# Products of constants on TensorE ahead of the recurrence and beside the first steps of the sample's group

## The chip, the cores and the metric

The kernel runs on one core of one Trainium2 chip. The metric is the device time of one execution in microseconds, from a few runs on the same chip; the median of the runs is compared. A profiled execution is separate from those runs and has a time of its own.

## The reference: what is computed

One inference step of an encoder trunk of two layers, for 512 prompt frames and 32 sample frames of 1024 channels that share the weights. Each layer:

```
p = rmsnorm(x) @ w_in                    # 1824 columns, shared by three mixers
A: gated linear recurrence over 256 channels (conv, gates, scan)
B: delta rule with a matrix state, 4 heads of 64 x 64
     S = S*w - (S kk)(kk a)' + v k' ;  y = S r
C: latent attention, 8 heads, latent of 128, one rotary key of 32,
   block-causal for the prompt, 256 cached keys for the sample
x += concat(A, B, C) @ w_out
x += cross-attention into 256 memory tokens, 4 heads of 256
x += squared-ReLU MLP, hidden 4096
```

The end is one more RMSNorm. Outputs are both groups' results and their new states and caches.

## The kernel before

All 544 frames are kept transposed in SBUF, and the big products go by weight tiles of 1024 x 128: a stream of 119 such tiles a layer (`in`, `out`, `mk`, `mv`, `mq`, `mo`, `f1`, `f2`) comes by DMA into a ring of three. ScalarE makes a rounded copy of each tile (`wH`), VectorE the remainder (`wL`), and TensorE takes every product as three (`three`: high by high, low by high, high by low), in two halves of 272 frames (`halves`). The order of each engine's work is written out by hand in the kernel, and semaphores couple the engines.

Between the stages `in` and `out` of each layer lies the stretch that the change touches. There TensorE's program is:

- the values (seven products with `W("uv")`) and the first keys (`project(2)`, `project(3)`, with `W("uk")`), all of plain f32 with up to 512 columns, through banks 4 and 5 of PSUM;
- then `weave(recurrence(), attention())`, which takes a step of the one or of the other by a string of turns.

`attention` runs over 40 units (head h, block b; block 4 of a head is the sample's 32 frames). It starts with two query projections (`project(0)`, `project(1)`: rows whose operands are `ringR`, since the ring's free buffers hold the rounded query weights), and has for each unit u a step with `score(u)` (`akH,aqH` and two more rows) and a step with a further projection and `turn(u - 1)`, the transposes of the normalised weights (`cst,aP`). VectorE and ScalarE rotate and split the queries (VectorE L1920 to L1930, ScalarE `aqH<-hT`) and make the softmax (VectorE L1954 to L1963, ScalarE `aP`).

`recurrence` is mixer B in chunks of 64 frames. The prompt's groups g = 0 to 3 have two chunks each, the sample's group is g = 4 (`NG - 1`) and has one. Two lanes of groups run beside each other; the sample's group is the first of lane 1, and for some steps it is alone. Its steps are `tokens` (eight transposes, L799 to L802), `score_l`, `score_m`, `merge` and `cross` over levels, `solve`, `blocks`, `state`. Ahead of them come five steps of TensorE's turn order in which it has nothing to do for the recurrence (`factor`), while ScalarE takes exponentials (`decays`, `ke`, `afr`, `bf`, `afr`) and VectorE makes the factors with them: L1793 to L1799, with the semaphore `factors` on the last, for which `tokens` waits.

The order string beside the factors, and the helper for a product:

```
BESIDE_FACTORS = ("", "aaa", "aaa", "a", "a")
...
            def mm(out, a, b, start=True, stop=True):
                return e.matmul(out, lhsT=a, rhs=b, start=start, stop=stop)
```

`C(name, a, b)` is a slice of the constants `cst`; `ident` is the identity matrix of 128 x 128 in it, and `reset` a row of zeros and ones, one zero in every 64. Bank 7 of PSUM holds `crossed`, the results of `cross`, later in the same stretch.

Of the kernel before, what the change touches and what calls it, by code (L numbers as in the profile page):

```python
# [19 lines left out]
NG = SEQ // GRP + 1  # L20
# [123 lines left out]
def chunks_of(g):  # L144
    return (0, 1) if g < NG - 1 else (0,)
# [14 lines left out]
def lane_of(g):  # L160
    return int(g in LANES[1])
# [25 lines left out]

BESIDE_FACTORS = ("", "aaa", "aaa", "a", "a")  # L190


def _turns():

    order = ""
    for i in range(ALONE):
        order += "r" + (BESIDE_FACTORS[i] if i < FACTOR_STEPS else "a" * (1 + i % 2))

# [34 lines left out]
def build(nc, wall, lw_d, vec_d, cst_d, x_d, mem_d, mks_d, mvs_d, outs):  # L233
# [5 lines left out]
    with ctx:  # L239
# [97 lines left out]
        def C(name, a, b, rows=slice(0, 128)):  # L337
            return cst[rows, CST[name] + a:CST[name] + b]
# [17 lines left out]
        ident, ones, bones = (C(n, 0, 128) for n in ("ident", "ones", "bones"))  # L356
# [11 lines left out]
        def bank(i, a=0, b=512):  # L368
            return PS[:, i * 512 + a:i * 512 + b]
# [20 lines left out]
        def at(l, name, i=1):  # L390

            return before.get(name, 0) + l * PER_LAYER[name] + i
# [12 lines left out]
        def bank_of(use):  # L405
            i = USES.index(use)
            return 4 + (i % 2 if i < FIRST else use[0] != "s")
# [78 lines left out]
        def akL(l, j):  # L486
            return akL1[:, :] if j else ringR[:, slot_of_out(l, 2), 0:KEYS]
# [12 lines left out]
        def nth(kind, g, b=0):  # L500

            mine = [step for step in REC_STEPS if step[0] == kind]
            return mine.index((kind, g, b)) + 1
# [143 lines left out]
        def _(e):  # L647
            def mm(out, a, b, start=True, stop=True):
                return e.matmul(out, lhsT=a, rhs=b, start=start, stop=stop)  # L649
# [132 lines left out]
            for l in range(DEPTH):  # L782
# [6 lines left out]
                def tokens(g):  # L789
                    x, n = lane_of(g), 64 * len(chunks_of(g))  # L790
                    cols = slice(GRP * g, GRP * g + n)
                    e.wait_ge(s["factors"], at(l, "factors"))
                    i = LANES[x].index(g)
                    if i:

                        p = LANES[x][i - 1]
                        e.wait_ge(s["y_out"], at(l, "y_out", nth("state", p, chunks_of(p)[-1])))
                    for t in range(2):
                        e.transpose(bank(2 * x, 128 * t, 128 * t + 128)[0:n, :], xs[:, 4 + t, cols], ident)  # L799
                        e.transpose(bank(2 * x, 256 + 128 * t, 384 + 128 * t)[0:n, :], afr[:, 0, t, cols], ident)  # L800
                        e.transpose(bank(2 * x + 1, 128 * t, 128 * t + 128)[0:n, :], be[:, t, cols], ident)
                        last = e.transpose(bank(2 * x + 1, 256 + 128 * t, 384 + 128 * t)[0:n, :], ke[:, t, cols],  # L802
                                           ident)
                    last.then_inc(s["tok_T"], 1)
# [4 lines left out]
                def score_l(g):  # L809
                    x = lane_of(g)  # L810
                    e.wait_ge(s["tok_out"], at(l, "tok_out", nth("tokens", g)))
                    for t in range(2):
                        for h, c in quads(g):
                            f = frames(g, c)
                            part(bank(2 * x + h, 128 * t, 128 * t + 128)[rows_of[c], :], bf[rows_of[h], t, f],
                                 afr[rows_of[h], :, t, f])
                    for t in range(2):
                        for h, c in quads(g):
                            f = frames(g, c)
                            last = part(bank(2 * x + h, 256 + 64 * t, 320 + 64 * t)[rows_of[1 - c], :],  # L820
                                        afr[rows_of[h], 0, t, f], bf[rows_of[h], t, f])
                    last.then_inc(s["score_l"], 1)

                def score_m(g):
                    x = lane_of(g)
                    e.wait_ge(s["score_l_out"], at(l, "score_l_out", nth("score_l", g)))
                    for t in range(2):
                        for h, c in quads(g):
                            f = frames(g, c)
                            last = part(bank(2 * x + h, 128 * t, 128 * t + 128)[rows_of[c], :], kf[rows_of[h], t, f],  # L830
                                        afr[rows_of[h], :, t, f])
                    last.then_inc(s["score_m"], 1)

                def cross(g, b):
                    x = lane_of(g)
                    e.wait_ge(s["merge_out"], at(l, "merge_out", nth("merge", g, b - 1)))
                    if nth("cross", g, b) > 1:

                        e.wait_ge(s["cross_out"], at(l, "cross_out", nth("cross", g, b) - 1))
                    for w in range(4):  # L840
                        for c in chunks_of(g):
                            r = rows_of[c]
                            last = part(crossed(x, 64 * w, 64 * w + 64)[rows_of[1 - c], :], LG[x][r, w, 0:64],
                                        XX[x][r, 0, w, :])
                    last.then_inc(s["cross"], 1)
# [70 lines left out]
                def state(g, c):  # L916
# [11 lines left out]
                            last = part(o[:, 384 + 64 * t:448 + 64 * t], src[r, t, :], rp[r, c, t, :], False)  # L928
                    last.then_inc(s["state_mm"], 1)

                def recurrence():
                    for kind, g, b in REC_STEPS:
                        if kind == "tokens":
                            tokens(g)
                        elif kind == "score_l":
                            score_l(g)
                        elif kind == "score_m":
                            score_m(g)
                        elif kind == "cross":
                            cross(g, b)  # L940
                        elif kind == "merge":
                            merge(g, b)
                        elif kind == "solve":
                            solve(g)
                        elif kind == "blocks":
                            blocks(g)
                        elif kind == "state":
                            state(g, b)
                        yield
# [49 lines left out]
                def score(u):  # L999
                    h, b = UNITS[u]  # L1000
                    if u == 0:
                        e.wait_ge(s["marks"], at(l, "marks"))
                    if b == 0:
                        e.wait_ge(s["q_out"], at(l, "q_out", 2 * h + 2))
                        e.wait_ge(s["k_out"], at(l, "k_out", 2 * h + 2))
                    wait_bank(e, l, ("s", u))
                    j = h % 2
                    if b < 4:
                        o, q, keys, rows = bank(bank_of(("s", u)), 0, 128 * b + 128), slice(128 * b, 128 * b + 128), \
                            slice(0, 128 * b + 128), slice(0, MKD)  # L1010
                    else:
                        o, q, keys, rows = bank(bank_of(("s", u)), 0, KEYS - SEQ)[0:DEC, :], slice(SEQ, T), \
                            slice(SEQ, KEYS), slice(0, QKD)
                    mm(o, aqH[rows, j, q], akH[rows, j, keys], True, False)
                    mm(o, aqH[0:QKD, j, q], akL(l, j)[0:QKD, keys], False, False)
                    mm(o, aqL[0:QKD, j, q], akH[0:QKD, j, keys], False, True).then_inc(s["a_score"], 1)
# [37 lines left out]

                def attention():

                    e.wait_ge(s["cq_lo"], at(l, "cq_lo"))
                    for p in range(2):
                        project(p)
                        yield  # L1060
                    for u, (h, b) in enumerate(UNITS):
                        score(u)
                        if u >= 2 and UNITS[u - 2][0] % 2:
                            weigh(u - 2)
                        yield
                        if h + 1 < HEADS and b < (2 if h % 2 == 0 else 4):
                            project(4 * (h + 1) + b)
                        if u in NORM_UNITS:
                            norm_early(NORM_UNITS.index(u))
                        if u:  # L1070
                            turn(u - 1)
                        yield
                    turn(len(UNITS) - 1)
                    weigh(len(UNITS) - 2)
                    yield
                    weigh(len(UNITS) - 1)
# [1177 lines left out]
```

## Time and profile before

| what | value |
|---|---|
| median of 3 runs | 1940.93 us (1940.87 to 1943.75) |
| the profiled execution's own time | 1937.82 us |
| its span, first to last instruction | 1935.7 us |
| mean granted TensorE clock | 0.966 of full speed |
| TensorE busy (matmul) | 1813.7 us (94%) |
| VectorE busy | 1020.1 us (53%) |
| ScalarE busy | 724.9 us (37%) |
| GpSimd busy | 105.2 us (5%) |

The columns of TensorE's rows are start, busy time, engine, line, operands and tiles; the clock of a stretch stands as a share of full speed (1.00 is 2.4 GHz, 0.50 is 1.2 GHz). A product of plain f32 stands in the trace as two matmul rows. Line L649 is that of the helper `mm`, so products are told apart by their tiles. Times are from the span's start. Layer 0's stretch between `in` and `out` runs from 129 to 335 us, layer 1's from 1081 to 1287 us.

### The profile page before, as it was taken

The page shows a single profiled execution, that of the slowest core. Times are in us where ns is not written, and L with a number is a line of the kernel's source. Part 1 is how long each engine was busy: PE and PEld are TensorE (multiplying, and loading weights), DVE is VectorE, ACT ScalarE, POOL GpSimd, SP SyncE. Part 2 cuts the span into 40 slices and gives each one's busy share as a digit, 9 for nine tenths or more (in the row PEclk, how much of TensorE's full clock was granted, in tenths as well). Part 3 has the DMA queues.
Part 4 walks back from the last instruction along what each step waited for, and adds up shares of the span by engine and source line. Part 5 has one row for each costly group of instructions (what it writes and reads, how often), then busy time and mean ns, then how long its engine had stood idle before and what let it go on. Part 6 is the DMA issues. An engine that isn't in the chain of part 4 may idle for free.

```text
span 1935.7 us, 37571 instructions
## 1 busy us (share of the span) xinstructions
PE 1813.7 (94%) x16534; PEld 1699.3 (88%) x16534; DVE 1020.1 (53%) x1741; ACT 724.9 (37%) x1268; POOL 105.2 (5%) x108
## 2 busy tenths in 40 slices
PE   5996988999999999999999789889999999999997
PEld 5975777999889999999999567779987999999996
DVE  6677665554435544344367776655443455353533
ACT  4434555463334212121335355554433422121212
POOL 2020000200010000000100100001000100000001
PEclk9997998999999999999999789999999999999998
DMA  5200000553122222222221000133510222222221
GB/s 218 75 10 1 4 24 25 194 173 116 34 77 77 88 89 87 90 86 91 84 77 55 8 3 2 35 111 119 198 46 32 80 95 88 88 88 88 88 88 58
DMA packets 38593, 149.51 MB, mean 77 GB/s; under 512 B 4384, under 2 KB 4544, under 8 KB 36768
## 3 DMA queue, kind: packets, MB, share of 16 engines
q1 hardware_dynamic: 36288, 131.05, 20.4%
q0 software_dynamic: 2144, 16.06, 2.2%
q8 instruction: 131, 2.15, 0.5%
q14 instruction: 30, 0.25, 0.0%
HBM read 139.68 MB, written 7.41 MB: 76 GB/s over the span
## 4 chain that ended last, share of the span: by engine, by line
PE 85%; DVE 7%; ACT 4%; issue 1%; POOL 1%; DMA 1%; DVEq 0%; ACTq 0%; SPq 0%; POOLq 0%
PE PS L649 78%; PE PS L787 5%; PE PS L1026 1%; DVE stat L1954 1%; ACT hH L1166 1%; ACT aP L1166 1%; POOL sq L575 1%; DVE rs L1921 0%; DVE hT L1920 0%; PE PS L1122 0%; DVE hL L1607 0%; DVE hT L1923 0%; ACT akH L1166 0%; ACT L1166 0%; DVE kf L1780 0%
## 5 line engine op out<-in xcount | busy, mean ns | idle before, releaser
L649 PE MATMUL PS<-hH,wH 128*128 128x272 f32 x2272 | 492.1, 298 | 33.7 <-DMA cst<-cst_in 16.9
L649 PE MATMUL PS<-hH,wL 128*128 128x272 f32 x2272 | 476.7, 291 | 0.0
L649 PE MATMUL PS<-hL,wH 128*128 128x272 f32 x2272 | 476.0, 291 | 0.0
L1593 DVE TENSOR_TENSOR wL<-ring,wH 128x1024 fp32r<-128x1024 f32 x238 | 301.0, 1265 | 216.9 <-ACT wH L1166 216.6
L649 PEld LDWEIGHTS PS<-hH,wH 128*128 128x128 f32 x2272 | 361.5, 190 | 50.5 <-issue 19.1
L1166 ACT ACTIVATE wH<-ring 128x1024 fp32r<-128x1024 f32 x238 | 249.8, 1051 | 333.8 <-PE PS L649 333.8
L649 PEld LDWEIGHTS PS<-hH,wL 128*128 128x128 f32 x2272 | 362.4, 191 | 0.0
L649 PEld LDWEIGHTS PS<-hL,wH 128*128 128x128 f32 x2272 | 360.3, 191 | 0.0
L649 PE MATMUL PS<-hidH,wL 128*128 128x272 f32 x1024 | 212.0, 288 | 0.0
L649 PE MATMUL PS<-hidH,wH 128*128 128x272 f32 x1024 | 211.7, 288 | 0.0
L649 PE MATMUL PS<-hidL,wH 128*128 128x272 f32 x1024 | 211.1, 288 | 0.0
L1619 DVE TENSOR_TENSOR xT<-PS,xT 128x544 f32<-128x544 f32 x96 | 69.4, 723 | 241.8 <-PE PS L649 241.6
L649 PEld LDWEIGHTS PS<-hidH,wH 128*128 128x128 f32 x1024 | 161.0, 188 | 0.0
L649 PEld LDWEIGHTS PS<-hidL,wH 128*128 128x128 f32 x1024 | 160.9, 189 | 0.0
L649 PEld LDWEIGHTS PS<-hidH,wL 128*128 128x128 f32 x1024 | 159.8, 189 | 0.0
L1166 ACT ACTIVATE hidH<-hid 128x544 fp32r<-128x544 f32 x64 | 42.2, 659 | 281.2 <-DVE hid L2085 281.2
L575 POOL TENSOR_TENSOR sq<-sq 128x544 f32<-128x544 f32 x49 | 68.1, 1389 | 1113.3 <-ACT sq L1166 1113.3
L2083 DVE TENSOR_TENSOR hid<-PS,rs 128x544 f32<-128x544 f32 x64 | 46.3, 724 | 114.3 <-PE PS L649 106.2
L1166 ACT ACTIVATE sq<-xT 128x544 f32<-128x544 f32 x56 | 36.8, 657 | 178.9 <-DVE xT L1619 174.3
L1954 DVE TENSOR_REDUCE stat<-PS 128x1 f32<-128x256 f32 (+5 forms) x120 | 55.0, 458 | 71.9 <-PE PS L649 70.3
L1166 ACT ACTIVATE aP<-PS,stat 128x128 f32<-128x128 f32 (+4 forms) x80 | 41.4, 517 | 80.1 <-DVE stat L1955 79.8
L1602 DVE SCALAR_TENSOR_TENSOR hL<-xT,vec,hH 128x544 fp32r<-128x544 f32 x48 | 43.1, 921 | 11.7 <-ACT hH L1166 11.5
(320 smaller groups left out, 2554.9 us busy)
## 6 DMA issues: line engine op xcount, KB each, us to landing
ring<-wall SPq DMA_DIRECT2D x238, 512.0 KB, 3.3
lw<-lw_in POOLq DMA_DIRECT2D x2, 2240.0 KB, 10.2
xT<-x_in SPq DMA_DIRECT2D x4, 544.0 KB, 7.2
y_out<-hT SPq DMA_DIRECT2D x8, 272.0 KB, 2.1
mem<-mem_in POOLq DMA_DIRECT2D x2, 1024.0 KB, 5.0
mks<-mks_in POOLq DMA_DIRECT2D x2, 1024.0 KB, 10.2
mvs<-mvs_in POOLq DMA_DIRECT2D x2, 1024.0 KB, 13.3
memk_out<-mkp POOLq DMA_DIRECT2D x2, 1024.0 KB, 6.1
```

Source lines behind the costliest of these rows:

```text
L575: e.tensor_tensor(sq[:, 0, :], sq[:, 0, :], sq[:, 1, :], ALU.add).then_inc(s["sq_added"], 1)
L649: return e.matmul(out, lhsT=a, rhs=b, start=start, stop=stop)
L787: return e.matmul(out, lhsT=a, rhs=b, start=start, stop=True, skip_group_check=True)
L1026: last = e.transpose(bank(6, 128 * j, 128 * j + 128), aP[:, u % 2, 128 * j:128 * j + 128], ident)
L1166: return e.activation(out, in_, f, **kw)
L1593: tt(wL[:, n % SPLIT], ring[:, n % RING], plain(wH[:, n % SPLIT]), ALU.subtract).then_inc(w_lo, 1)
L1602: stt(hL[:, k, :], xT[:, k, :], V(l, gain, k), plain(hH[:, k, :]), ALU.mult, ALU.subtract)\
L1619: tt(xT[:, k, :], ps, xT[:, k, :], ALU.add).then_inc(evac["dve"], 1)
L1954: link(e.reduce_max(stat[0:n, 16 + u % 2:17 + u % 2], bank(scores, 0, nk)[0:n, :], AX))
L2083: tt(m, ps, rs, ALU.mult).then_inc(evac["dve"], 1)
```

## The change

A helper `keep_busy(n)` issues n products of `ident` with the 512 columns of `reset` into bank 7. They wait for nothing and signal nothing, and nobody reads their result. They stand at these places of each layer, on TensorE alone: five ahead of the first query projection, three ahead of `score(0)`, two ahead of `score(2)`, eight ahead of `tokens` of the sample's group, one ahead of `score(3)`, two ahead of `score(4)`, and two ahead of `score_m` of the sample's group: 23 products a layer, 46 in all.

```
+KEEP_BUSY = {0: 3, 2: 2, 3: 1, 4: 2}
...
+                def keep_busy(n):
+
+                    for _ in range(n):
+                        mm(bank(7), ident, C("reset", 0, 512))
+
                 def recurrence():
                     for kind, g, b in REC_STEPS:
+                        if (kind, g) == ("score_m", NG - 1):
+                            keep_busy(2)
                         if kind == "tokens":
+                            if g == NG - 1:
+                                keep_busy(8)
                             tokens(g)
...
                 def attention():
 
+                    keep_busy(5)
                     e.wait_ge(s["cq_lo"], at(l, "cq_lo"))
                     for p in range(2):
                         project(p)
                         yield
                     for u, (h, b) in enumerate(UNITS):
+                        if u in KEEP_BUSY:
+                            keep_busy(KEEP_BUSY[u])
                         score(u)
```

The first place is TensorE's program of layer 0 where the weave begins: `lw` is the last key product, `ringR` the first query projection. Before:

```order
L649 MATMUL PS<-ckv,lw 128x512
L649 MATMUL PS<-ckv,lw 128x32
L649 MATMUL PS<-lw 128x256
L649 MATMUL PS<-ringR 128x272
L649 MATMUL PS<-cqL,ringR 128x272
```

And now:

```order
L651 MATMUL PS<-ckv,lw 128x512
L651 MATMUL PS<-ckv,lw 128x32
L651 MATMUL PS<-lw 128x256
L651 MATMUL PS<-cst 128x512 x5
L651 MATMUL PS<-ringR 128x272
L651 MATMUL PS<-cqL,ringR 128x272
```

Five products (the rows with `cst` alone) stand between the keys and the projections; nothing else has moved.

The second place is TensorE's program of layer 0 from the turn of unit 1 (`cst,aP`, two blocks) to `score_m` of the sample's group (`afr,kf`); `cst,xs` to `cst,ke` are its `tokens`, `afr,bf` and `bf,afr` its `score_l`. Before:

```order
L1026 MATMUL PS<-cst,aP 128x128 x2
L799 MATMUL PS<-cst,xs 64x128
...
L802 MATMUL PS<-cst,ke 64x128
L649 MATMUL PS<-akH,aqH 128x512
...
L1026 MATMUL PS<-cst,aP 128x128 x3
L787 MATMUL PS<-afr,bf 64x128 x4
L787 MATMUL PS<-bf,afr 64x64 x4
L649 MATMUL PS<-akH,aqH 32x288
L649 MATMUL PS<-ringR,aqH 32x288
L649 MATMUL PS<-akH,aqL 32x288
L787 MATMUL PS<-afr,kf 64x128 x4
```

And now:

```order
L1037 MATMUL PS<-cst,aP 128x128 x2
L651 MATMUL PS<-cst 128x512 x8
L801 MATMUL PS<-cst,xs 64x128
...
L804 MATMUL PS<-cst,ke 64x128
L651 MATMUL PS<-cst 128x512
L651 MATMUL PS<-akH,aqH 128x512
...
L1037 MATMUL PS<-cst,aP 128x128 x3
L789 MATMUL PS<-afr,bf 64x128 x4
L789 MATMUL PS<-bf,afr 64x64 x4
L651 MATMUL PS<-cst 128x512 x2
L651 MATMUL PS<-akH,aqH 32x288
...
L651 MATMUL PS<-akH,aqL 32x288
L651 MATMUL PS<-cst 128x512 x2
L789 MATMUL PS<-afr,kf 64x128 x4
```

Here too the old rows keep their order; eight, one, two and two products stand between them.

## Rows read from the trace of the kernel before

**Rows 1.** Stretches: length, busy us of PE, PEld, DVE, ACT, POOL; granted clock.

```profile
129.00:174.70 45.70, 27.33 (x126) 18.04 (x125) 37.56 (x68) 19.02 (x41) 7.66 (x8) 0.66 0.03 8
174.70:327.30 152.60, 136.97 (x2537) 112.00 (x2536) 95.47 (x283) 81.18 (x223) 1.16 (x2) 0.97 0.05 14
...
1081.40:1126.90 45.50, 27.16 (x125) 17.86 (x123) 37.57 (x68) 19.02 (x41) 7.67 (x8) 0.66 0.03 8
```

**Rows 2.** PE's waits by releaser, 129 to 163 us: total, times, longest.

```profile
PE PS L649 <- DVE ringR L1948: 4.8, 1, 4.8
PE PS L649 <- DVE aqL L1930: 2.5, 1, 2.5
PE PS L649 <- ACT aP L1166: 1.4, 1, 1.4
```

**Rows 3.** PE's waits by releaser, 163 to 175 us.

```profile
PE PS L799 <- DVE afr L1799: 7.2, 1, 7.2
PE PS L787 <- DVE P L1808: 1.5, 1, 1.5
PE PS L649 <- ACT aP L1166: 0.6, 1, 0.6
```

**Rows 4.** Stretches, columns as in rows 1: the waits, and what lies between.

```profile
129.20:137.50 8.30, 8.30 (x22) 2.90 (x20) 7.96 (x8) 4.76 (x9) 5.56 (x7) 1.00 0.13 44
137.50:142.30 4.80, 0.01 (x2) 0.04 (x1) 4.72 (x9) 1.40 (x3) 2.10 (x2) 0.76 0.00 0
142.30:156.30 14.00, 9.73 (x36) 8.24 (x36) 9.50 (x25) 6.58 (x13) 0.00 (x0) 0.50 0.00 1
163.50:167.10 3.60, 3.60 (x14) 2.79 (x14) 2.88 (x7) 1.07 (x2) 0.00 (x0) 0.50 0.02 5
167.10:170.80 3.70, 1.60 (x23) 0.85 (x23) 3.09 (x9) 1.79 (x5) 0.00 (x0) 0.96 0.00 0
170.80:174.10 3.30, 3.30 (x23) 2.49 (x23) 2.26 (x8) 1.47 (x5) 0.00 (x0) 0.50 0.00 0
```

**Rows 5.** Timeline of PE: start, busy us, line, tiles, count, wait before.

```profile
129.19 4.73 PE L649 MATMUL PS<-lw,ckv 128*128 128x512 f32 x10
133.85 1.98 PE L649 MATMUL PS<-lw 128*128 128x512 f32 x4
...
174.89 0.29 PE L649 MATMUL PS<-cqL,ringR 128*128 128x272 f32 x1
...
181.27 2.07 PE L649 MATMUL PS<-ckv,lw 128*128 128x512 f32 x2
183.13 0.63 PE L1026 MATMUL PS<-cst,aP 128*128 128x128 f32 x2
```

**Rows 6.** The chain of waits, 142 to 175 us, in order of time.

```profile
142.29 1.71 PE PS L649 x6
...
147.82 0.89 PE PS L649 x3
...
149.82 1.05 ACT ke L1166
...
154.04 0.46 ACT aP L1166 x2
...
170.61 1.08 PE PS L787 x8
...
173.27 1.47 PE PS L787 x16
```

**Rows 7.** Stretches where the clock is low later, columns as in rows 1.

```profile
181.00:184.30 3.30, 3.30 (x10) 1.95 (x9) 2.00 (x7) 1.83 (x5) 0.00 (x0) 0.50 0.00 0
...
324.00:327.80 3.80, 2.55 (x38) 2.02 (x35) 0.91 (x4) 1.41 (x6) 0.54 (x1) 0.99 0.05 17
327.90:341.20 13.30, 12.58 (x41) 9.29 (x38) 8.71 (x14) 10.99 (x16) 0.54 (x1) 0.50 0.11 41
...
1287.00:1290.00 3.00, 3.00 (x14) 3.00 (x15) 1.42 (x3) 2.99 (x6) 0.00 (x0) 0.50 0.00 0
```

## Prediction

> **What bounds the kernel now.** I read the stretches first, to see where TensorE is not full; then its waits there and who ended them; then its timeline, for what a product costs at either clock; and last the chain of waits through the stretch.
>
> TensorE is busy for 94% of the span, and nearly everywhere it is the bound. The reader should see the exception: in the 45.7 us between the stage `in` and the middle of the weave it is busy for 27.3 us only, at a mean granted clock of 0.66, while VectorE is busy for 37.6 us; layer 1 has the same stretch with the same numbers, 45.5 us and 0.66 [rows 1]. From there on, TensorE is busy for 137 of 152.6 us at 0.97.
>
> In that stretch five waits matter: 4.8 us for the keys' remainders (VectorE L1948), 2.5 us for the queries' (L1930), 1.4 us for a softmax [rows 2], 7.2 us for the last factor (L1799) and 1.5 us for L1808 [rows 3]. The clock tells the rest. In the 8.3 us of f32 products before the first wait it is 1.00; in the wait it falls, and it stays at 0.50 (1.2 GHz) over the whole of 142.3 to 156.3 us, also while TensorE works 9.7 of 14 us, and on through the 7.2 us wait. It rises to 2.4 GHz only at 167.1 us, after 3.6 us of closed work, is lost again at 170.8 us after a stretch with 1.6 us of work in 3.7, and is back at 174.1 us [rows 4]. So about 20 us of work run at half speed. Some of it lies on the chain that ends the stretch, and that part alone is worth anything.
>
> **The price of a product.** An added product is f32 with 512 columns and is two rows. Ten such rows last from 129.19 to the next start at 133.85 us, 0.466 each, so a product costs 0.93 us at 2.4 GHz. Two such rows at 1.2 GHz last from 181.27 to 183.13 us, so it costs 1.86 us there [rows 5]. 46 products are then 43 us of TensorE at full clock. They have cover only as far as TensorE would have waited.
>
> **Step 1, five products in the first wait.** 5 x 0.93 = 4.65 us in a wait of 4.8 us [rows 2] that starts while the clock is 1.00. VectorE's chain to L1948 needs nothing of TensorE, so the first projection starts as before, at 142.3 us; cost nothing. The gap left is about 0.1 us, so the clock has no wait to fall in.
>
> **Step 2, from there to `tokens`, at full clock.** The six matmuls of the first projection take 1.71 us on the chain [rows 6], 0.285 each with their overlap. At full clock a 272-column row follows the next in 0.125 us instead of 0.227 (the start at 174.89 has neighbours at that distance, its own length is 0.29 [rows 5]), so they end about 0.8 us earlier. The three rows of `score(0)`, 0.89 us on the chain [rows 6], give 0.2 to 0.3 more: 1.0 us. That is the start of ScalarE's exponentials. They and the softmax behind them run from 149.8 to 154.5 us without a gap that TensorE ends [rows 6], and VectorE takes the factors without a wait: no further gain, no loss. So `factors` and with it `tokens` come at 162.5 us instead of 163.5 us. Cover for the other products here: three (2.8 us) in the wait of 2.5 us, which grows to about 3 since the projections end sooner; two (1.9 us) in the wait of 1.4 us plus 1.0 us that the rows ahead save; eight (7.44 us) in the wait of 7.2 us. TensorE reaches these eight about 1.9 us earlier than before and `factors` only 1.0 us earlier, so the wait would be about 8.1 us, and 0.6 us is spare. Cost nothing, unless the clock is low.
>
> **Step 3, the sample's first steps at full clock.** `tokens` takes 0.9 instead of 1.7 us, ending at 163.4. One product brings 164.3, `score(3)` (512 columns) 165.0, the turn of unit 2 165.4, `score_l` 166.0; ScalarE's copies of the tokens are ready by 164.8. Two products follow, to 167.9; `score(4)` needs a softmax that would be ready at about 166.9, so here 1.0 us of fill lies on TensorE's own chain. `score(4)` ends at 168.3, two more products at 170.2. L1808, for which `score_m` waits, follows the softmax of unit 3 through VectorE and would now end at about 168.9 instead of 170.6 us [rows 6]: fill costs 1.2 us here. `score_m` starts at 170.2 instead of 170.6 us, only 0.4 us sooner. From there to the end of the first `merge` the old kernel needs 174.7 - 170.6 = 4.1 us, nearly all at 0.50 [rows 4, 6]; at full clock the eight, four and three rows and the sixteen of the merge are some 1.9 us shorter, of which VectorE's L1815 between them leaves 1.8. Gain at that point: 0.4 + 1.8 = 2.2 us.
>
> **The sum.** 2.2 us a layer, in step with what stands behind it, since TensorE is the bound there [rows 1]; two layers give 4.4 us. Against the profiled execution's 1937.82 us that is 1933.4 us. The runs' median lies 3.1 us above the profiled one, so the same sum against 1940.93 us gives **1936.5 us**.
>
> Bounds of what I can't read: the clock after 175 us. It falls again at 181.0 us, for 3.3 busy us [rows 7], which costs 1.6 us; at 327.9 us, where f32 products and the first weight tiles run at 0.50 for 12.6 busy us, against 3.0 us in layer 1 [rows 7]. Half of the difference is 4.8 us on paper, 2.4 us by what the gaps between the products give back. The change moves the work against these falls without a plan. Each can go or come: from 2.4 us lost to 1.6 + 2.4 = 4.0 us won. I take 0, since the layers show both cases, and keep these ends for the range.
>
> **A rule that speaks against it.** The clock is lost in this kernel without any long wait too: at 170.8 us after 1.6 us of work in 3.7 us, and at 327.9 us after 2.6 us in 3.8 [rows 4, 7]. This is what the Trainium skill says on its page "TensorE: Matmul & The Clock Gate", section "A second HAM failure mode: psum-queue depth-cycling": frequent short idle pieces between groups of matmuls let the clock swing, though no single wait is long. By that rule the added products hold the clock only while they stand close, and step 3's gain shrinks. It is the second case below. The trace agrees so far that short waits cost the clock at 170.8 us.
>
> **The rivals.**
> - *The clock is held up to `tokens` but not in the sample's steps.* For it: the fall at 170.8 us, and that the small products there are of 64 x 64. Against it: with five added products the stretch from 162.5 to 170.2 us has no wait above 0.3 us. Then step 2's 1.0 us stays, and step 3 loses its 1.8 us and pays 1.2 us of fill, less the 0.6 us that `tokens` and `score_l` save: about 0.6 us a layer, 1939.7 us.
> - *The later falls go too.* 1.6 us twice, or the 2.4 us of layer 0's end once, on top of the forecast: 1932.5 to 1934.5 us. For it: the falls depend on where the thin pieces come, and these move. Against it: the pieces behind 175 us are unchanged.
> - *The products do not hold the clock* (the other side). Their operands are an identity and ones; no row shows such a product at length. If only useful data counted, the clock would fall during the first wait as now. Price: five products end at about 144.3 instead of 142.3 us (+2.0), three take 5.6 us in 2.5 (+3.1), two take 3.7 in 1.4 (+2.3), eight 14.9 in 7.2 (+7.7 and the lateness of the 7.4 before it), five more 9.3 us over 2.1 us of waits (+7.2): about 22 us a layer, 1985 us; if the fill itself raises the clock after some us, a third of it, about 1955 us. It decides at the first projection: at 1.2 GHz there, this case holds. Against it: f32 products of the same shape hold 1.00 over 8.3 us [rows 4]. The same page says, in "What's actually happening", that the gate goes by how busy the array has been, which would rule this case out.
> - *The later falls turn out worse*: layer 1's end comes to look like layer 0's, +2.4 us in a layer or both, and one more fall: 1937 to 1943 us.
>
> **Chances.** Forecast 0.50 (its own range 1934 to 1939 us), first rival 0.20, later falls go 0.20, no hold 0.03, later falls worse 0.07. A measurement here can tell 0.2%, 3.9 us, from no change: below 1937.05 is faster, above 1944.8 slower. The forecast lies just inside faster: 0.37 of its 0.50; with 0.20 of the good case and a little of the bad, 0.58. Slower: 0.03, 0.02 of the last and as much for what I overlook, 0.07. Same: the rest, 0.35. The range leaves out the no-hold case and the tails: 1932 to 1941 us.
>
> **What would show it.** In the changed profile: granted clock 1.00 from 129 to at least 170 us (and 1081 to 1122); the first projection at 142.3 us still; `tokens` at 162.5 us; `score_m` at 170.2 us released by nothing but TensorE's own row; the first merge ending at 172.5 us; each added product at 0.93 us. Wrong, if the clock is 0.50 at the first projection, if `tokens` does not come sooner (then VectorE, not TensorE, sets all of it), or if the 2.2 us of the stretch is gone by the first `out` tile.

## The result, and the profile after

| | median | runs | ratio to before, 95% interval |
|---|---|---|---|
| before | 1942.34 us | 6 (1939.64 to 1946.28) | |
| changed | 1929.22 us | 6 (1925.53 to 1997.16) | 0.9933 (0.9916 to 0.9950) |

13.1 us are gained (0.7%), where 4.4 us were forecast, and 1929.2 us lies below the stated range. Of the 13.1 us, 1.4 are a kernel before that is slower in these six runs than in the three that the forecast started from (1940.93 us). The execution of 1997.16 us, which was also the first one profiled, had a granted clock near 0.85 over most of its span; the profile read here is that of the first run below (e1), the same kernel at 1924.83 us, with a span of 1922.7 us and a mean clock of 0.990. It is the fastest of the four profiles of the changed kernel that are used here (the others took 1928.4 to 1932.8 us), which agree up to the middle of the weave and differ behind it.

The stretch between `in` and the weave of the changed kernel, with the columns of [rows 1]:

```profile
129.00:171.80 42.80, 39.46 (x164) 20.05 (x164) 36.84 (x66) 18.56 (x39) 7.66 (x8) 1.00 0.03 9
171.80:328.40 156.60, 137.61 (x2573) 111.91 (x2568) 101.16 (x295) 87.42 (x234) 1.16 (x2) 1.00 0.05 17
1074.60:1117.40 42.80, 39.48 (x165) 20.06 (x165) 36.98 (x67) 18.55 (x39) 7.67 (x8) 1.00 0.03 9
```

The clock is 1.00 in both layers' stretches, where [rows 1] have 0.66, and in this profile it is 1.00 to the end of layer 0's weave as well. Its waits from 129 to 172 us, against [rows 2, 3]:

```profile
PE PS L651 <- ACT aP L1180: 1.3, 2, 1.0
PE PS L801 <- DVE afr L1813: 1.1, 1, 1.1
PE PS L651 <- issue: 0.9, 2, 0.5
```

Of some 18 us of waits 3 are left. The timeline of TensorE, the added products (rows `cst` alone, two rows each) and their neighbours:

```profile
137.31 4.46 PE L651 MATMUL PS<-cst 128*128 128x512 f32 x10
142.15 0.37 PE L651 MATMUL PS<-ringR 128*128 128x272 f32 x1 [0.39 <-issue]
...
154.21 7.03 PE L651 MATMUL PS<-cst 128*128 128x512 f32 x16
162.30 0.30 PE L801 MATMUL PS<-cst,xs 128*64 128x128 f32 x1 [1.05 <-DVE afr L1813]
...
167.98 1.88 PE L651 MATMUL PS<-cst 128*128 128x512 f32 x4
169.79 0.65 PE L789 MATMUL PS<-afr,kf 64*64 64x128 f32 x8
...
172.29 0.39 PE L651 MATMUL PS<-ringR 128*128 128x272 f32 x1
```

Sixteen rows take 7.03 us, so a product costs 0.88 us. The first projection starts at 142.15 us, `tokens` at 162.3, `score_m` at 169.8, and the first merge is over at 172.3 us. The forecast had 142.3, 162.5, 170.2 and 172.5 us. So its steps 1 to 3 came out within 0.4 us, and the missing 9 us lie elsewhere.

### The profile page after: what moved, and what is told of

Same layout as the page of the kernel before. It is cut to its first block, busy times and chain, and to the rows that moved or that the text cites. A ratio compares the mean times of both kernels' runs of the same rounds, so it can differ in the third digit from the quotient of the medians.

```text
span 1995.0 us, 37755 instructions
## 1 busy us (share of the span) xinstructions
PE 1911.0 (96%) x16626; PEld 1758.6 (88%) x16626; DVE 1020.3 (51%) x1741; ACT 725.8 (36%) x1268; POOL 105.2 (5%) x108
## 4 chain that ended last, share of the span: by engine, by line
PE 89%; DVE 4%; ACT 4%; issue 1%; POOL 1%; DMA 0%; DVEq 0%; SPq 0%; ACTq 0%; POOLq 0%
PE PS L651 82%; PE PS L789 5%; PE PS L1037 1%; ACT hH L1180 1%; POOL sq L577 1%; DVE stat L1968 1%; PE PS L1136 0%; DVE hL L1621 0%; DVE rs L1935 0%; DVE hT L1934 0%; ACT aP L1180 0%; ACT L1180 0%; POOL msq L629 0%; DVE wL L1607 0%; DMA mem<-mem_in 0%
## 5 line engine op out<-in xcount | busy, mean ns | idle before, releaser
L651 PE MATMUL PS<-hH,wH 128*128 128x272 f32 x2272 | 508.6, 307 | 32.2 <-DVE hL L1616 23.0
L651 PE MATMUL PS<-hH,wL 128*128 128x272 f32 x2272 | 488.7, 298 | 0.0
L651 PE MATMUL PS<-hL,wH 128*128 128x272 f32 x2272 | 488.3, 298 | 0.0
L651 PEld LDWEIGHTS PS<-hH,wH 128*128 128x128 f32 x2272 | 372.1, 194 | 51.9 <-issue 20.5
L651 PEld LDWEIGHTS PS<-hH,wL 128*128 128x128 f32 x2272 | 370.3, 193 | 0.0
L651 PEld LDWEIGHTS PS<-hL,wH 128*128 128x128 f32 x2272 | 369.3, 193 | 0.0
L651 PE MATMUL PS<-hidH,wH 128*128 128x272 f32 x1024 | 216.6, 294 | 0.0
L651 PE MATMUL PS<-hidL,wH 128*128 128x272 f32 x1024 | 216.4, 293 | 0.0
L651 PE MATMUL PS<-hidH,wL 128*128 128x272 f32 x1024 | 216.2, 294 | 0.0
L2097 DVE TENSOR_TENSOR hid<-PS,rs 128x544 f32<-128x544 f32 x64 | 46.4, 725 | 125.4 <-PE PS L651 116.8
L1968 DVE TENSOR_REDUCE stat<-PS 128x1 f32<-128x256 f32 (+5 forms) x120 | 54.9, 458 | 78.5 <-PE PS L651 77.2
L1616 DVE SCALAR_TENSOR_TENSOR hL<-xT,vec,hH 128x544 fp32r<-128x544 f32 x48 | 43.2, 922 | 11.6 <-ACT hH L1180 11.4
```

What stands on the lines that cost most here:

```text
L1616: stt(hL[:, k, :], xT[:, k, :], V(l, gain, k), plain(hH[:, k, :]), ALU.mult, ALU.subtract)\
L1968: link(e.reduce_max(stat[0:n, 16 + u % 2:17 + u % 2], bank(scores, 0, nk)[0:n, :], AX))
L2097: tt(m, ps, rs, ALU.mult).then_inc(evac["dve"], 1)
```

## The experiments

In all of them the kernel before ran beside the others on the same chip. Three points of TensorE's program serve as marks in every layer: the starts of `score` of unit 8 and of unit 22 (three rows each, the first `akH,aqH`, with 512 columns for unit 8 and 384 for unit 22), and the start of the first weight tile of stage `out`. Each is counted from the first row `lw,ckv` at the end of stage `in`, called the stage's end below.

**e1, the change again.**

> The change as it is, once more, for a second set of times and another profile. Theory A (the gain sits in the stretch from 129 to 175 us and its twin, and was mis-sized there): the first merge of the sample's group ends over 5 us earlier than before's 174.7 us, and the rest of each layer is as long as before. Theory B (the stretch gives about 2.2 us a layer as worked out, the rest comes from falls of the clock after 175 us that no longer happen): the merge ends near 172.5 us, and the lowered pieces after it (before: 181, 300, 311, 328 and 356 us in layer 0) are fewer. Both: ratio 0.993.

Measured: 1929.7 us, 0.9935 (0.9918 to 0.9952). Theory A falls: the merge ends at 172.3 us. B is borne out in this profile: of the stretches at 0.50 behind 175 us that the first profile of before has in layer 0, those at 181 [rows 7], 300 and 311 us are absent, and up to there only the one at 328 us is left.

**e2, e3 and e4, parts of the change.** e2:

```
-KEEP_BUSY = {0: 3, 2: 2, 3: 1, 4: 2}
+KEEP_BUSY = {0: 3, 2: 2}
...
-                        if (kind, g) == ("score_m", NG - 1):
-                            keep_busy(2)
```

> Leaves out the five products beside the sample's steps (one, two and two). Theory A: tokens come at 162.5 us; by my sum the five cost 2.2 us of fill and bring 1.8 us, so about the same gain as the whole change, within 1 us a layer. Theory B: if the clock is lost in the sample's steps the later falls are as before, and the ratio goes back to about 0.998.

Measured: 0.9995 (0.9980 to 1.0011). The eighteen products ahead of `tokens` hold the clock and bring `tokens` forward exactly as in e1 (33.14 us behind the stage's end), and the first merge ends 0.5 us behind e1's in layer 0 and 0.9 us in layer 1 (43.7 and 44.1 us behind the stage's end, against 43.2), still 1.4 to 1.9 us sooner than in the kernel before. Yet the kernel is no faster than before. Its profile shows why:

```profile
162.00:165.00 3.00, 1.49 (x22) 0.88 (x21) 2.45 (x7) 1.74 (x5) 0.00 (x0) 1.00 0.00 0
165.00:168.30 3.30, 1.75 (x15) 1.00 (x15) 3.08 (x8) 1.47 (x5) 0.00 (x0) 1.00 0.00 0
168.50:185.40 16.90, 16.84 (x94) 12.33 (x94) 9.36 (x28) 6.20 (x18) 0.00 (x0) 0.50 0.00 1
```

TensorE works about half the time from 162 to 168 us, the clock goes to 1.2 GHz, and it stays there for 17 us in which TensorE is busy without a pause. In layer 1 it is the same, and unit 22 comes at 110.5 us in both layers.

e3 is the other half:

```
+KEEP_BUSY = {3: 1, 4: 2}
...
-                            if g == NG - 1:
-                                keep_busy(8)
...
-                    keep_busy(5)
```

> Keeps only the five products beside the sample's steps and leaves out the eighteen ahead of tokens. Clock at 1.2 GHz until about 167 us as before, tokens at 163.5 us. Theory A: no gain, 0.5 to 1.5 us a layer of fill on TensorE's chain, ratio 1.000 to 1.0015. Theory B: if these five are what keeps the clock later on, ratio 0.996 or below.

Measured: 0.9964 (0.9950 to 0.9977). Five products a layer, which make the first merge no earlier than before (it ends 45.5 and 46.4 us behind the stage's end, against 45.5), win some 7 us. Theory A gave them a loss. The clock comes back 37 and 39 us behind the stage's end, inside the sample's steps, and is not lost in them again; unit 22 comes at 107.9 and 108.7 us.

e4 leaves out the eight products alone:

```
-                            if g == NG - 1:
-                                keep_busy(8)
```

> Leaves out the eight products in the 7.2 us wait for the factors alone. The clock holds until about 155 us, is lost in the wait, and the sample's steps run at 1.2 GHz until it rises: Theory A: the 1.0 us of step 2 stays, the five later products cost up to 2 us each pair at the low clock, ratio 0.999 to 1.003. Theory B: the later falls come back too, the same ratio or worse.

Measured: 0.9968 (0.9955 to 0.9981). Both theories expected a slower kernel than this. The clock is lost in the wait for the factors (at 0.50 from 159 to 169 us) as expected, but `tokens` keeps its gain (33.13 us), and the sample's steps have no low stretch of 17 us. Unit 22 comes at 109.0 us.

**e5, e6, e7 and e12, more profiles of the unchanged kernels.**

> The kernel before, unchanged, for another profile. Theory B1 (the later falls of the clock are placed by the way the clock rises at the end of the low stretch, so the same in every execution): low near 181, 300 and 311 us in layer 0 and at the same distances behind tokens in layer 1, as in the first profile. Theory B2 (they are chance, and the first profile was unlucky): other places, fewer of them.

> The changed kernel, unchanged, for another profile. Theory B1: no low clock between 129 and 328 us or 1 to 2 pieces at places that differ from profile to profile. Theory B2: 2 to 4 pieces in each layer, at places that differ.

> As the one before: a third profile of the changed kernel, to see whether the places of the low pieces repeat.

> The kernel before, for a third profile: whether the low stretch of 17 us from 170 to 188 us is the usual case (then score of unit 22 starts 112.0 us behind the stage's end) or the short one of the first profile is (108.9 us).

The second profile of the kernel before (e5, 1943.71 us), stretches with the columns of [rows 4]:

```profile
163.50:167.10 3.60, 3.60 (x28) 2.75 (x28) 2.85 (x7) 1.07 (x2) 0.00 (x0) 0.56 0.02 5
167.10:170.60 3.50, 1.30 (x22) 0.73 (x15) 2.92 (x8) 1.79 (x5) 0.00 (x0) 0.92 0.00 0
170.80:174.20 3.40, 3.40 (x27) 2.58 (x24) 1.92 (x7) 1.64 (x5) 0.00 (x0) 0.50 0.00 0
174.20:181.00 6.80, 6.80 (x47) 5.91 (x46) 3.44 (x10) 2.01 (x7) 0.00 (x0) 0.50 0.00 0
181.00:187.60 6.60, 6.60 (x32) 4.04 (x28) 3.71 (x11) 2.83 (x7) 0.00 (x0) 0.54 0.00 0
...
1126.50:1143.50 17.00, 16.94 (x99) 12.43 (x98) 9.49 (x27) 6.44 (x19) 0.00 (x0) 0.52 0.00 1
```

Up to 170.8 us this is the picture of [rows 4]; but where the clock came back at 174.1 us there, here it stays at 0.50 to 187.7 us, in both layers. The third profile (e12, 1947.79 us) has the same 17 us in both layers. So four of the six layers profiled have it, and the one profile that the forecast was worked from, the fastest of the three at 1937.82 us, has it in neither.

| us from the end of `in` | score of unit 22 | first `out` tile |
|---|---|---|
| before, first profile, layers 0 and 1 | 109.0, 108.9 | 206.2, 205.4 |
| before, e5 | 112.0, 112.0 | 208.2, 209.5 |
| before, e12 | 112.1, 112.0 | 209.7, 209.4 |
| changed, e1, e6, e7, e14 (8 layers) | 105.5 in each | 199.0 to 203.2 |

The rows for unit 22 in layer 0 of the first profile of before, then of e5, then of e1 (the stage ends at 129.19, 129.20 and 129.17 us):

```profile
238.16 0.42 PE L649 MATMUL PS<-akH,aqH 100*128 100x384 f32 x1
```

```profile
241.23 0.42 PE L649 MATMUL PS<-akH,aqH 100*128 100x384 f32 x1
```

```profile
234.72 0.42 PE L651 MATMUL PS<-akH,aqH 100*128 100x384 f32 x1
```

None of these four profiles of the changed kernel has a low clock between 129 and 188 us or at that place of layer 1; the eight layers reach unit 22 within 0.04 us of each other. Further on neither B1 nor B2 holds. The changed kernel too has low pieces at three places of a layer, near 240, 295 to 302 and 305 to 312 us by the times of layer 0: e6 has the later two in both layers, e14 one of them in layer 0 and both in layer 1, e7 all three in layer 0 and the first in layer 1, e1 none. The kernel before has two or three such pieces in each of its six layers, in the second layers of e5 and e12 one of them at another place.

**e8, fewer products in the sample's steps.** e2 with the two products ahead of `score_m` kept.

> Keeps the eighteen products ahead of tokens and the two ahead of score_m, and leaves out the three beside unit 3 and 4. The wait before score_m was where the clock was lost without any of the five (thin from 165 to 168.5 us). If the two alone hold the clock, the low stretch of 17 us goes, and the ratio is 0.993 or better, since about 1 us of fill a layer is saved. If they don't (the work of 163 to 166 us stays thin), the clock is lost near 168 us in most executions and the ratio is 0.997 to 1.000.

Measured: 1929.3 us, 0.9935 (0.9918 to 0.9952), unit 22 at 104.8 us in both layers: two products in place of five save 0.8 us a layer and hold the clock here. The same kernel again, as e16:

> The kernel of e8 again: 0.9935 as before, 0.7 us a layer ahead of e14 up to unit 22, which the noise of the times hides.

Measured: 1931.22 us, 0.9935 (0.9921 to 0.9950). In layer 0 the clock is low from 167 to 170 us, and unit 22 comes at 106.2 us. Over the twelve layers profiled with this pair alone (e8, e11, e13, e15, e16, e18) that happened in four, layer 0 each time, and it costs 1.4 us; with all five products it happened there in none of ten (e1, e6, e7, e14, e17). The three further products buy this for 0.8 us a layer, which comes to about nothing on the mean (1.4 us in four of twelve layers is 0.5 us).

**e9, as many products, an eighth of the columns.**

```
-                        mm(bank(7), ident, C("reset", 0, 512))
+                        mm(bank(7, 0, 64), ident, C("reset", 0, 64))
```

> The 23 products of a layer stay where they are, but with 64 columns instead of 512: as many instructions, an eighth of the work, at most 0.25 us each. If it is the closed work that holds the clock, it is lost in the first wait and in the 7.2 us wait as before, and the time is that of before: ratio 0.999 to 1.002. If some activity in the waits is enough, whatever its amount: tokens 33.1 us behind the last stage's end and 0.993.

Measured: 1936.95 us, 0.9987 (0.9966 to 1.0007), with times from 1931 to 1947 us. Two stretches of its profile:

```profile
140.60:154.00 13.40, 11.00 (x50) 10.27 (x49) 9.72 (x25) 6.58 (x13) 0.00 (x0) 0.53 0.01 2
154.00:161.00 7.00, 3.11 (x15) 2.92 (x16) 6.95 (x8) 1.78 (x5) 0.00 (x0) 0.50 0.00 0
```

As many instructions stand at the same places, and the clock is lost at 141 us: it is the products' length that counts, not their presence. Whether the short ones do nothing at all is not shown. Neither layer of this profile has the low stretch of 17 us, the median lies 5.5 us below that of the kernel before beside it, and the interval of the ratio allows both no gain and 0.3%.

**e10, the pair behind the thin piece.** e2 and

```
-KEEP_BUSY = {0: 3, 2: 2}
+KEEP_BUSY = {0: 3, 2: 2, 5: 2}
```

> The eighteen products ahead of tokens, none in the sample's thin piece, and two just behind it (ahead of score(5)). If the two products ahead of score_m work by keeping the clock from being lost there, these come too late: lost near 168 us. If all that counts is to get it back, the low stretch of 17 us shrinks to 3.4 or 7 us. Ratio between those of e2 and e8: 0.996 to 0.999. If the clock plays no part in the step, 0.999 to 1.000 as e2.

Measured: 0.9959 (0.9942 to 0.9976), between e2 and e8. The clock is lost near 167 us in layer 0 and at the same place of layer 1, the low stretch lasts 6.8 us instead of 17, and unit 22 comes at 109.0 and 108.7 us, where e2 has 110.5. The added rows run at the low clock:

```profile
170.61 3.62 PE L651 MATMUL PS<-cst 128*128 128x512 f32 x4
```

In this profile the clock is back behind the long products in both layers, where in e2 it stayed low through 17 us of small work without a pause. That e10's ratio lies below e2's agrees; two layers of each are little evidence for more. To keep the clock, as e8 does, is worth 4 us a layer more up to unit 22.

**e11, e13, e15: two later waits.** To e8 come one product ahead of `blocks` of group 0 and one ahead of `norm_squares`, each in a wait of TensorE for ScalarE, into a bank that is free there:

```
+                        if (kind, g) == ("blocks", 0):
+                            keep_busy(1)
...
                     if i == 0:
                         wait_bank(e, l, ("g", 1))
+                        keep_busy(1, 5)
```

> As e8 (eighteen ahead of tokens, two ahead of score_m), and one product in each of two later waits: ahead of blocks of group 0 (1.5 us wait for ScalarE's copy) and ahead of norm_squares (1.7 us). Each product lies in its wait and costs nothing. If the falls near 243 us and near 300 us come from these two waits, they go: about 1.4 us each in the executions that have them, 2 to 5 us for the kernel, ratio 0.991. If the thin work around them is what does it, no change against e8: 0.9935.

> The kernel of e11 again, beside the others on the same chip. If the two later products win what e11 showed: ratio 0.991, and below e14's and e16's by 0.002 or more; no low clock near 240 us and near 300 us in the profile. If e11 was chance: as e16.

> The changed kernel, for comparison on the same chip: ratio 0.9935. Its profile: score of unit 22 at 105.5 us behind the stage's end, the later falls at 240, 300 or 310 us in some layers.

> As e8 with the one product ahead of blocks of group 0, without the one ahead of norm_squares. If each later fall hangs on the wait beside it: the fall near 240 us is gone (unit 23 at 7.76 us behind unit 22 in every layer), those near 300 us stay, ratio between e13's and e16's.

Measured: e11 1923.65 us, 0.9909 (0.9887 to 0.9931); e13, the same kernel, 1923.35 us, 0.9892 (0.9875 to 0.9909); on the same chip e14, the changed kernel, 1929.21 us, 0.9919 (0.9902 to 0.9935), and e15 1927.13 us, 0.9916 (0.9898 to 0.9934). The wait ahead of `norm_squares` in e14 and the stretches around it in layer 0:

```profile
293.29 1.10 PE L651 MATMUL PS<-rstd_early,cst 128*128 128x256 f32 x4 [1.67 <-ACT rstd_early L1180]
```

```profile
291.00:294.00 3.00, 1.33 (x12) 1.09 (x7) 1.32 (x5) 1.54 (x5) 0.00 (x0) 1.00 0.00 0
294.00:297.50 3.50, 3.50 (x54) 3.00 (x52) 0.42 (x1) 1.37 (x4) 0.00 (x0) 0.55 0.02 5
```

and in e13:

```profile
292.33 1.07 PE L651 MATMUL PS<-cst 128*128 128x512 f32 x2
294.08 1.13 PE L651 MATMUL PS<-rstd_early,cst 128*128 128x256 f32 x4 [0.67 <-ACT rstd_early L1183]
```

```profile
291.00:294.00 3.00, 2.40 (x47) 1.51 (x41) 1.65 (x6) 2.36 (x7) 0.00 (x0) 1.00 0.02 5
294.00:297.50 3.50, 3.42 (x59) 2.80 (x60) 0.45 (x2) 1.76 (x6) 0.00 (x0) 1.00 0.00 0
```

One product of 0.88 us in a wait of 1.67 us keeps the clock there. The eight layers profiled with it (e11, e13, e17, e18) have no low piece between 285 and 320 us or at that place of layer 1; of the twelve that have the five products or the pair in the sample's steps but nothing in either later wait (e1, e6, e7, e14, e8, e16), nine have one. e15, which fills only the earlier wait, was expected to keep these pieces and has none in its one profile. But three of its six times lie at 1924.5 to 1925.3 us with a mean clock of 0.989 (the profiled one is of these) and three at 1928.9 to 1931.9 us with 0.983, as if the pieces came in half of its executions; no profile of a slower one shows it. For the fall near 240 us the evidence is thin: of those twelve layers one first and three second layers have it, and of the ten with the product ahead of `blocks` none at the place itself; e18 has one some 20 us further on, in layer 1.

**e17 and e18.** The changed kernel with all 23 products and the two later ones (e17), beside the kernel of e13 (e18).

> The changed kernel with all its 23 products a layer, and the two later ones of e13. In the profiles so far the three products that e13 leaves out cost 0.75 us a layer, but without them the clock was lost near 167 us in 3 of 10 layers, at 1.4 us. So against e18 about 0.3 us a layer slower, within the noise: ratio 0.989 to 0.991, no low clock between 129 and 320 us.

> The kernel of e13, a third time, beside e17: ratio 0.989 to 0.991, low clock near 167 us in some layer, none near 240 and 300 us.

Measured: 1923.93 us, 0.9902 (0.9886 to 0.9917), and 1925.55 us, 0.9906 (0.9892 to 0.9920). They can't be told apart, as expected. Not as expected, e17 has one low piece in the sample's steps of layer 1, at 1122 us, a place where no other profile with its products has one; unit 22 comes at 106.5 us there instead of 105.5. So the five products don't hold the clock there in every execution. Both kernels beat the kernel before by 1.0%; on one chip (e13 against e14) the two later products and the leaner pair together beat the changed kernel by 5.9 us.

## Why the prediction was wrong

*Steps 1 and 2* held: 142.15 against 142.3 us, 162.3 against 162.5 us. A product took 0.88 us, not 0.93. The rival that such products don't hold the clock is refuted by the clock of 1.00 over 42.8 us.

*Step 3* held in its numbers. The gain at the merge is 2.35 us against the first profile. The fill delays `score_m` by 1.1 us against e2 (40.6 against 39.5 us behind the stage's end; the forecast had 1.2), and even so the merge ends 0.5 to 0.9 us sooner than in e2. My expectation of e2, that the five products cost 2.2 us up to the merge and bring 1.8, was wrong: the 1.0 us ahead of `score(4)` is not added to the 1.2 at `score_m` but lies in it. Where the account went wrong is that it ended at the merge.

*The sum* is the step that failed, in "2.2 us a layer, in step with what stands behind it", together with the bound behind it: "Each can go or come ... I take 0". What the runs showed in its place is 5.5 us a layer up to unit 22. Between the merge and unit 8 the changed kernel gains again in all eight layers, because it keeps the clock. Against the first profile that is 1.2 us a layer: unit 8 starts 54.2 us behind the stage's end there and 50.7 in the changed kernel, a difference of 3.5 against 2.3 at the merge. Against e5 and e12 the difference at unit 8 is 57.3 - 50.7 = 6.6 us or a tenth less, of which 2.3 to 2.4 at the merge: 4.2 us behind it. From unit 8 to unit 22 both kernels take 54.7 to 54.9 us in every layer.

Of the 17 us at 0.50, 11.7 lie between the merge and unit 8. The same piece of e5 and of e1, and the one wait that e1 has in it:

```profile
174.76:186.48 11.72, 11.72 (x65) 8.80 (x63) 6.67 (x19) 3.75 (x12) 0.00 (x0) 0.50 0.00 0
```

```profile
172.29:179.84 7.55, 6.86 (x65) 5.17 (x63) 6.03 (x18) 3.79 (x14) 0.00 (x0) 1.00 0.01 2
177.05 0.44 PE L651 MATMUL PS<-akH,aqH 100*128 100x384 f32 x1 [0.56 <-ACT aP L1180]
```

At full clock the piece takes 7.55 us and not half of 11.72, which is 5.86. 0.7 us of the difference is time in which TensorE stands, 0.56 of it a wait for ScalarE's softmax. The other 1.0 us is busy time of the same 65 rows that the clock doesn't halve: 6.86 us.

With four of six layers of that kind, the kernel before reaches unit 22 at 111.0 us on the mean, the changed one at 105.5: 5.5 us a layer, 11.0 in all. From unit 22 to the first `out` tile the six and eight layers take 97.1 and 96.0 us on the mean, which makes 2.2 us more for two layers, but that mean hangs on where single low pieces lie. Together 13.2 us, and 13.1 were measured; that the two agree to the tenth is luck, since the share of layers with the long stretch comes from three profiles.

The reading that went wrong before the sum: the profile was 3.1 us faster than the median of the runs, and I carried the sum over to the median as if the two differed by noise. They differed by a mechanism in the very stretch that the change touches, so the change was worth more on the median than on the profile. The mark was in [rows 4]: the clock comes back after 3.6 us, is lost and comes back again, and what changes so often in one execution can go otherwise in the next; it should be priced both ways. The range had for this only "later falls go too", with 1.6 us twice; the price of a low stretch longer than the profile's was in none of my cases.

*The rule of the Trainium skill* that I set against the change, in "TensorE: Matmul & The Clock Gate", section "A second HAM failure mode: psum-queue depth-cycling", says that frequent short idle pieces between groups of matmuls let the clock swing, and that throughput suffers by it. The traces agree for the old kernel and e2: the clock is lost at 171 and 168 us with no wait above 1.5 us in the sample's steps. I drew the wrong conclusion for the change. The rule speaks against it only if the products leave such waits, and e1 has none from 162.3 to 172.3 us; what the swing costs the kernel before, 1.2 or 4.2 us a layer behind the merge, I didn't ask. My rival from it gave 1939.7 us; its own terms, 1.0 + 0.6 - 1.2, make 0.4 us a layer and not 0.6, so 1940.1 us.

What stays open: why the same small work lets the clock come back after 3.3 us in one execution and not in 17 us in another. The profiles show both for the same instructions, and no run here changed what may decide it. The 2.4 us that the forecast took for the end of layer 0 "by what the gaps between the products give back" no run measured by itself.

## What to carry to other kernels

Where a trace shows TensorE's clock lost in a stretch of short waits and small matmuls, price the whole stretch up to where the clock is safely back, at its longest, and from several profiles, before pricing any single wait; if the profile is faster than the median, ask what the slower executions have in the stretch under change. A product that nobody reads is cheap where it fits a wait (0.88 us in 1.5 us or more), and the longest waits are not the first places to fill: five products beside the thin work won 7 us, eighteen in the long waits ahead of it alone won nothing. On top of the five the same eighteen were worth 5 to 6 us (0.9935 against 0.9964), since their gain was then not lost again behind them. Give the products enough columns: at an eighth of the length no gain clear of noise was left.

## What the runs showed that I had not expected

- TensorE busy without a pause for 17 us at 1.2 GHz (16.90 of 16.90 us in e5's stretch from 170.8 to 187.7 us), made of small f32 matmuls, transposes and some of 272 to 512 columns, without the clock rising. A busy share of 1.00 can stand beside a clock of 0.50.
- The same kernel has executions with and without that stretch: 29 runs of before beside e1 span 1936.6 to 1946.5 us, with mean clocks of 0.968 to 0.960, the fast ones at the high clock. The fourteen runs of the kernel of e11, e13 and e18 span 1921.1 to 1926.8 us: with the clock held in more places the times also spread less.
- Products of an identity by zeros and ones hold the clock: 1.00 from 129.0 to 171.8 us, in the stretch that had 0.66.
